# Three products of rounded and low parts in place of a plain fp32 product, in two recurrence steps of seven heads

## The reference

```python
S = exp(b_last)[..., None] * S + einsum('bhsk,bhsv->bhkv', kc * exp(b_last - bcum), vc)   # keys by values
o = einsum('bhts,bhsv->bhtv', A, vc) + einsum('bhtk,bhkv->bhtv', qc * exp(bcum), S)       # scores by values + queries by state
o = rms_norm(o, g_onorm);  y = (o * silu(z)) @ w_out
```

## Time and profile before

| | |
|---|---|
| median of 3 runs | 1036.03 us (1035.98 to 1036.13) |
| the profiled execution, its own time | 1035.79 us |
| its span in the trace | 1033.9 us |
| TensorE busy | 1025.0 us, 99% |
| VectorE busy | 705.3 us, 68% |
| ScalarE busy | 425.8 us, 41% |
| granted TensorE clock, mean | 0.999 |

### The profile page before, as it was taken

The page is one execution under the profiler, slowest core; times in us unless marked ns, Lnnn a source line. Parts: engine busy times, 40 slices in busy tenths (PEclk is TensorE's granted clock), DMA queues, the critical chain, the costliest instruction groups (busy, mean ns, idle before and its releaser), DMA issues.

```text
span 1033.9 us, 20543 instructions
## 1 busy us (share of the span) xinstructions
PE 1025.0 (99%) x7979; PEld 976.8 (94%) x7979; DVE 705.3 (68%) x1274; ACT 425.8 (41%) x860; POOL 18.3 (2%) x45
## 2 busy tenths in 40 slices
PE   8999999999999999999999999999999999999998
PEld 7999999999999978889999999999999999997886
DVE  6899777677776926762867768485776848586355
ACT  7444333332433614443345444434534344383222
POOL 1000000000000000000000000000000000000000
PEclk9999999999999999999999999999999999999999
DMA  8003121112111243321112211211221122143064
GB/s 253 22 22 82 42 77 46 41 43 79 41 41 61 102 164 119 123 82 42 49 55 64 62 28 56 63 54 48 62 61 41 42 63 61 57 152 111 23 241 171
DMA packets 95552, 78.75 MB, mean 76 GB/s; under 512 B 2965, under 2 KB 86886, under 8 KB 95510
## 3 DMA queue, kind: packets, MB, share of 16 engines
q1 hardware_dynamic: 77622, 69.19, 21.2%
q10 hardware_dynamic: 17888, 8.98, 3.0%
HBM read 64.72 MB, written 13.44 MB: 76 GB/s over the span
## 4 chain that ended last, share of the span: by engine, by line
PE 98%; DVE 1%; DMA 1%; ACT 0%; issue 0%; SPq 0%; DVEq 0%
PE bank L678 36%; PE bank L728 28%; PE bank L816 14%; PE bank L703 5%; PE bank L1066 4%; PE bank L910 2%; PE bank L1022 1%; PE bank L1015 1%; PE bank L1024 1%; PE bank L926 1%; PE bank L798 1%; PE bank L918 1%; PE bank L1010 1%; PE bank L833 1%; PE bank L974 1%; PE bank L905 1%
## 5 line engine op out<-in xcount | busy, mean ns | idle before, releaser
L678 PE MATMUL bank<-reg_a,wsplit 128*128 128x352 f32 x2304 | 381.5, 324 | 0.0
L678 PEld LDWEIGHTS bank<-reg_a,wsplit 128*128 128x128 f32 x2304 | 368.6, 188 | 1.1
L728 PE MATMUL bank<-reg_a,wsplit 128*128 128x264 f32 x1344 | 165.7, 284 | 0.0
L728 PEld LDWEIGHTS bank<-reg_a,wsplit 128*128 128x128 f32 x1344 | 164.1, 188 | 0.2 <-DVE arena L1901 0.2
L728 PE MATMUL bank<-reg_b,w_ring 128*128 128x264 f32 x1008 | 124.6, 284 | 0.0
L728 PEld LDWEIGHTS bank<-reg_b,w_ring 128*128 128x128 f32 x1008 | 123.3, 188 | 0.0
L816 PE MATMUL bank<-reg_b,reg_a 128*128 128x512 f32 x288 | 69.3, 396 | 0.0
L816 PEld LDWEIGHTS bank<-reg_b,reg_a 128*128 128x128 f32 x288 | 53.7, 188 | 12.6 <-issue 0.4
L1929 DVE TENSOR_TENSOR arena<-arena,bank 128x264 f32<-128x264 f32 x84 | 34.8, 427 | 34.2 <-PE bank L728 33.0
L1288 ACT ACTIVATE arena<-bank 128x264 f32<-128x264 f32 x84 | 32.2, 390 | 55.2 <-PE bank L728 50.5
L1266 ACT ACTIVATE w_ring<-wraw 128x512 fp32r<-128x512 f32 x42 | 26.1, 631 | 69.0 <-PE bank L728 69.0
(11 more groups left out here) (299 smaller groups left out, 1498.6 us busy)
## 6 DMA issues: line engine op xcount, KB each, us to landing
wraw<-in_w_in SPq DMA_DIRECT2D x64, 512.0 KB, 4.1
first_x<-in_x_prompt SPq DMA_DIRECT2D x8, 512.0 KB, 8.4
wraw<-in_w_out SPq DMA_DIRECT2D x8, 512.0 KB, 3.5
w_out_raw<-in_w_out SPq DMA_DIRECT2D x8, 512.0 KB, 5.2
arena<-in_w_out SPq DMA_DIRECT2D x8, 512.0 KB, 4.7
arena<-in_x_prompt SPq DMA_DIRECT2D x8, 512.0 KB, 3.4
x_scratch<-arena SPq DMA_DIRECT2D x8, 512.0 KB, 2.6
arena<-in_state_hgrn ACTq DMA_DIRECT2D x8, 512.0 KB, 3.9
```

Of the source, the lines that this page charges most:

```text
L678: mm = nc.tensor.matmul(bank[b][:, 0:CH], w[wi][:, k, :], rhs[hi], start=(k == 0 and i == 0), stop=(k == KT - 1 and i == 2))
L728: mm = nc.tensor.matmul(bank[banks[q]][:, 0:QT], w[wi][:, k, :], B_OP[name][hi][:, k, q * QT:(q + 1) * QT], start=(start and k == 0 and i ...
```

## The change

For the seven heads of the loop, the eight keys-by-values products of step 9 and the eight scores-by-values products of step 10 become three float32r matmuls each. The queries-by-state products (L1024) stay plain fp32, and so does the whole last head. The rounded parts are written by ScalarE, the low parts by VectorE, into columns of the arena that are done with at that point (an alias `rounded` of the arena as float32r, and three functions that give the place of a chunk's two parts). New events tell of them: `kta`, `kt`, `vha`, `vhb`, `aha`, `ahb` of ScalarE and `kla`, `klb`, `vla`, `vlb`, `ala`, `alb` of VectorE (k keys, v values, a scores). The scores are split in two pieces: chunks 0 and 1 (`EARLY`) in step 8, the other six in step 9, where their rounded parts take the place of the keys' rounded parts.

```diff
+        rounded = nc.alloc_sbuf_tensor_at("arena_rounded", [P, ARENA], F32R, offset=arena_at)
+        AT_KT, AT_K = CK * P, (2 * CK + 1) * P
...
+        EARLY = 2
...
+            def three_terms(dst, w, x, stop):
+                for i, (wi, xi) in enumerate(((0, 0), (1, 0), (0, 1))):
+                    mm = nc.tensor.matmul(dst, w[wi], x[xi], start=(i == 0), stop=(stop and i == 2))
+                return mm
...
+                elif s == 9 and not final:
+                    for c in range(CK):
+                        if c % 4 == 0:
+                            pe.wait_ge(VR.sem, VR.at(h, ("vla", "vlb")[c // 4]))
+                        mm = three_terms(bank[5 + c // 4][:, tokens(c % 4)], split_keys(c), split_values(c), True)
+                    mm.then_inc(PR.now("u"), 1)
...
-                        mm = nc.tensor.matmul(dst, r_am[:, tokens(c)], r_vt[:, tokens(c)], start=True, stop=(c == 0))
+                        if final:
+                            mm = nc.tensor.matmul(dst, r_am[:, tokens(c)], r_vt[:, tokens(c)], start=True, stop=(c == 0))
+                        else:
+                            if c == EARLY:
+                                pe.wait_ge(VR.sem, VR.at(h, "alb"))
+                            mm = three_terms(dst, split_scores(c), split_values(c), c == 0)
...
+                elif s == 8 and not final:
+                    act.wait_ge(PR.sem, PR.at(h, "kt"))
+                    for half in range(2):
+                        A(rounded[:, AT_KT + half * 512:AT_KT + (half + 1) * 512], bank[5 + half][:, :],
+                          ACT.Copy).then_inc(AR.now(("kta", "kt")[half]), 1)
+                    for half in range(2):
+                        A(rounded[:, AT_K + half * 512:AT_K + (half + 1) * 512], r_vt[:, half * 512:(half + 1) * 512],
+                          ACT.Copy).then_inc(AR.now(("vha", "vhb")[half]), 1)
+                    act.wait_ge(moved32, h + 1)
+                    A(rounded[:, AT_F + T - EARLY * P:AT_F + T], r_am[:, 0:EARLY * P], ACT.Copy).then_inc(AR.now("aha"), 1)
+                elif s == 9 and not final:
+                    act.wait_ge(PR.sem, PR.at(h, "u"))
+                    A(rounded[:, AT_KT:AT_KT + (CK - EARLY) * P], r_am[:, EARLY * P:], ACT.Copy).then_inc(AR.now("ahb"), 1)
...
+            def low_part(dst, src, hi):
+                return V.tensor_tensor(dst, src, hi.bitcast(F32), ALU.subtract)
```

More of the change, by code:

```diff
@@ L219, in build, with part_at, split_keys, split_values @@
         r_qb = sb("r_qb", [P, (2 * NB + 1) * NS])
+        rounded = nc.alloc_sbuf_tensor_at("arena_rounded", [P, ARENA], F32R, offset=arena_at)
+        AT_KT, AT_K = CK * P, (2 * CK + 1) * P
+        AT_Q = AT_K + T
+        AT_F, AT_KR = AT_Q + T, AT_Q + 3 * T
+        AT_VT = AT_Q + 6 * T
+        EARLY = 2
+        def part_at(at):
+            return rounded[:, at:at + P]
+        def split_keys(c):
+            return part_at(AT_KT + c * P), part_at(AT_F + CH + c * P if c < 3 else AT_KR + CH + (c - 3) * P)
+        def split_values(c):
+            return part_at(AT_K + c * P), part_at(AT_VT + c * P)
+        def split_scores(c):
+            return part_at(AT_F + T - (EARLY - c) * P if c < EARLY else AT_KT + (c - EARLY) * P), part_at(c * P)
         STK = 3 * NSAMP
@@ L328, in build @@
         GATED = ["lb", "v3", "qc", "k", "fa", "f", "tt", "g4", "g3", "ri", "i3", "i2", "i1", "kq", "vl", "vs"]
-        ENDED = [f"s{c}" for c in range(CK)] + ["r0", "r1", "rs", "on0", "on1", "ons"]
+        STATES = [f"s{c}" for c in range(CK)]
+        ENDED = ["r0", "r1", "rs", "on0", "on1", "ons"]
+        LOWS = ["kla", "klb", "vla", "vlb", "ala"]
         VR = Events(sem("rec_dve"), GATED + ["u2", "w4", "u4", "qb", "k3c", "kl", "as", "w8", "u8", "w16", "u16", "am", "w32", "c8",
-                                             "u32", "ss", "sn0", "snew", "w64", "c16", "u64"] + ENDED,
+                                             "u32", "ss", "sn0", "snew", "w64", "c16", "u64"]
+                    + LOWS + STATES + ["alb"] + ENDED,
                     GATED + ["u2", "am", "as", "w4", "u4", "qb", "k3c", "w8", "c8", "u8", "kl", "w16", "c16", "u16",
-                             "w32", "u32", "ss", "sn0", "snew", "w64", "u64"] + ENDED)
-        AR = Events(sem("rec_act"), ["gc", "vh", "vt", "sv", "kts", "qr", "kr", "os", "sqs", "q32", "k32", "kt", "sq0", "sq1", "sd"],
+                             "w32", "u32", "ss", "sn0", "snew", "w64", "u64"] + STATES + ENDED)
+        AR = Events(sem("rec_act"), ["gc", "vh", "vt", "sv", "kts", "qr", "kr", "os", "sqs", "q32", "k32", "kta", "kt",
+                                          "vha", "vhb", "aha", "ahb", "sq0", "sq1", "sd"],
                     ["gc", "vh", "vt", "sv", "kts", "os", "sqs", "q32", "k32", "kt", "sq0", "sq1", "sd"])
@@ L2403, in rec @@
                     join(h, 64, tl, tr)
+                elif s == 8 and not final:
+                    dve.wait_ge(AR.sem, AR.at(h, "kta"))
+                    low_part(rounded[:, AT_F + CH:AT_F + CH + 3 * P], bank[5][:, 0:3 * P], rounded[:, AT_KT:AT_KT + 3 * P])
+                    low_part(part_at(AT_KR + CH), bank[5][:, 3 * P:], part_at(AT_KT + 3 * P)).then_inc(VR.now("kla"), 1)
+                    dve.wait_ge(AR.sem, AR.at(h, "kt"))
+                    low_part(rounded[:, AT_KR + CH + P:AT_KR + CH + 5 * P], bank[6][:, :],
+                             rounded[:, AT_KT + 512:AT_KT + 1024]).then_inc(VR.now("klb"), 1)
+                    for half in range(2):
+                        dve.wait_ge(AR.sem, AR.at(h, ("vha", "vhb")[half]))
+                        cols = slice(half * 512, (half + 1) * 512)
+                        low_part(rounded[:, AT_VT:AT_VT + CK * P][:, cols], r_vt[:, cols],
+                                 rounded[:, AT_K:AT_K + CK * P][:, cols]).then_inc(VR.now(("vla", "vlb")[half]), 1)
+                    dve.wait_ge(AR.sem, AR.at(h, "aha"))
+                    low_part(rounded[:, 0:EARLY * P], r_am[:, 0:EARLY * P],
+                             rounded[:, AT_F + T - EARLY * P:AT_F + T]).then_inc(VR.now("ala"), 1)
                 elif s == 9:
@@ L2417, in rec @@
                         ins.then_inc(VR.now(f"s{c}"), 1)
+                    if not final:
+                        dve.wait_ge(AR.sem, AR.at(h, "ahb"))
+                        low_part(rounded[:, EARLY * P:CK * P], r_am[:, EARLY * P:],
+                                 rounded[:, AT_KT:AT_KT + (CK - EARLY) * P]).then_inc(VR.now("alb"), 1)
                 elif s == 10:
```

## The result

| | before | changed |
|---|---|---|
| median | 1036.01 us (4 runs) | 1048.2 us (4 runs, 1047.39 to 1048.54) |
| ratio to before | | 1.012, 95% interval 1.0108 to 1.0133 |
| the profiled execution, its own time | 1035.79 us | 1047.39 us |
| its span | 1033.9 us | 1045.5 us |

The change costs 12.2 us by the medians. The profiled execution is the shortest of the four, so its span grew by only 11.6.

The account below looks back on a forecast made before the run. TensorE's own work was taken as the bound almost everywhere. Steps 9 and 10 each add 0.86 us a head, +12.0 us over seven heads with the rest hidden, so 1036.03 becomes 1048.0 us; range 1046.0 to 1052.0, holding 0.84.

Parts of the forecast that it names:

- The price of a rounded matmul at 128 columns: TensorE, steps 9 and 10: 0.110 us each, set by the weight load; +0.86 us a step, +12.0 us in all.
- the line through the wide forms: Busy time over count at 264, 352 and 512 columns, carried down: streaming alone would take 0.060 us at 128 columns.
- The step before the change: Step 9's 16 plain records, taken off as 1.78 us, 0.111 us a record.
- The hidden work: Splitting by ScalarE and VectorE in steps 8 and 9: fits in their idle time and costs nothing.
- the late scores: Low part of the later scores in step 10: ready before TensorE asks, margin 0.4 to 0.5 us, the thinnest.
- The edges of the runs: TensorE's passages between plain and rounded runs: taken as nothing, at most 0.05 us a run, 0.7 us for 14 runs.
- A sign that I named wrongly: TensorE's matmul records: shorter than 275 ns at the same 0.11 us distance would be the mark of a load bound.
- Streaming as the bound: Rival in steps 9 and 10: loads run ahead freely, 0.060 us a matmul, -4.8 us, 1031.2 us; chance 0.05.
- Partly hidden loads: Rival in steps 9 and 10: load begins before its predecessor is through, pace say 0.084, +3.3, 1039.3 us; chance 0.05.
- The waits: Rival: late low or rounded parts stop TensorE some 0.5 us a head, +3.5 us, 1051.5 us; chance 0.08.
- The narrow form: Rival: a narrow rounded matmul works in two records like plain fp32, +50 us, 1086 us; chance 0.06.

Follow-up runs that it names:

- half a load: Changed kernel, but step 9's 24 rounded matmuls each load only 64 of 128 weight columns and stream all 128; 1040.1 us.
- half a stream: Changed kernel, but step 9's 24 rounded matmuls each stream only 64 of 128 columns, weights staying 128 x 128; 1048.28 us.
- the bf16 kernel: Changed kernel with rounded and low parts written as bf16 instead of float32r, same three terms with fewer digits; 1032.49 us, ratio 0.997 to the kernel before.
- splitting alone: Changed kernel with all parts and waits made, but each product one plain fp32 matmul of the rounded parts; 1036.01 us, ratio 1.0002 to the kernel before.

## Why the prediction was right

*The price of a rounded matmul at 128 columns* was the whole of it. It was taken from places in the trace where loads follow each other with little streamed between, and not from the length of a record, its busy time or the line through the wide forms. It was put at 0.110; the loads lie 0.112 apart, and the steps last 2.63 us (2.64 forecast) and 4.16 (4.2). 16 records of 0.111 in seven heads are 12.4 us; the medians differ by 12.2. The experiments with half a load and half a stream show the cause, and not just the size.

*The step before the change was read too long.* The 1.78 us that the prediction takes off run from the start of a matmul to the end of the next group's first load. From start to start, as the 2.63 are measured, step 9 took 1.70. By the starts of the loads, 1.83 us became 2.73: +0.90 a step where the forecast has +0.86, and 12.6 us in fourteen steps where it has 12.0. TensorE's busy time grew by just these 12.6. That 1048.0 met the median of 1048.2 so closely is in this part luck.

*Why a record costs what it did.* The prediction gives a rounded matmul and a plain record the same price, and the reason is not the same. The rounded one waits for its load. A plain one also streams for 0.11 us, twice as long as a rounded one over the same 128 columns. In the bf16 kernel a bf16 matmul behind a plain record starts 0.11 us after it, in all 42 places, although one bf16 matmul follows another after 0.056 and its own load had begun together with the plain record (load at 601.13, matmul at 601.24, above). In the kernel before, plain products with only eight weight columns, four side by side, take 0.11 us a round too (16 records in the 0.44 us from 576.33 to 576.77):

```profile
576.33 0.62 PE L947 MATMUL bank<-arena,r_qb 128*8 128x128 f32 x16
576.77 0.40 PE L950 MATMUL bank<-arena,r_as 128*8 128x128 f32 x8
```

So at 128 columns the stream of a plain record is as long as a load. That the two prices are equal is a coincidence of this size and does not carry over to wider products.

*The hidden work* stayed hidden, as splitting alone shows. ScalarE had 0.48 us to spare where I had 0.3, the late scores 0.55 where I had 0.4 to 0.5; one chunk less of lead used that up.

*The edges of the runs* cost nothing that the trace shows: the first load of the next group still follows the last one of step 9 by 0.11 us (599.39 to 599.50).

*A sign that I named wrongly:* I wrote that a load-bound matmul would show as a record shorter than 275 ns. It doesn't. Groups of the changed kernel:

```profile
L989 PE MATMUL bank<-arena_rounded 128*128 128x128 f32 x336 | 47.2, 276 | 0.0
L989 PEld LDWEIGHTS bank<-arena_rounded 128*128 128x128 f32 x336 | 42.7, 192 | 0.0
```

The matmul's record begins while its own load is still running and contains the rest of it. With half the load it is 222 ns, 54 less. With half the stream it stays at 273. A plain record is 275 ns long and has its long stream in it instead. So a length of 275 does not say by itself what bounds a matmul; a change of one of the two did.

*The rivals.* Streaming as the bound (1031.2) was refuted for four-byte weights, and came true for bf16. Partly hidden loads (1039.3) did not occur. The waits did not bite at `EARLY = 2`. The narrow form cost no second record.

The Trainium skill, "TensorE: Matmul & The Clock Gate", section LDWEIGHTS (loading the stationary operand), puts a load at its columns over 1.2 GHz, which makes 107 ns for 128 (an estimate), and names no type; the four-byte loads here agree with 112 and the bf16 loads, 0.02 apart, don't. The section Back-to-back issue gap of the same page gives 81 ns a matmul of 128 columns for sustained pairs; neither kind comes near it here (112 and 56 ns), and the measurement decides.

## What to carry to other kernels

Count the weight loads and not only the passes. A plain fp32 product is two loads and two streams, each stream twice as long as a rounded one; three rounded products are three loads and three short streams. They pay only where those streams hide the loads, and at 128 streamed columns they don't. By the rows here (two plain streams at some 1.7 ns a column in all, three loads at 0.336 us) the break would lie near 200 streamed columns; that is an estimate, and no run tried it. Read a load's price where nothing streams beside it. Where stationary tiles are used once and narrow, two-byte parts hide the loads behind even 128 columns, if their digits suffice; then keep them apart from four-byte products, since each change back exposes half a load.

## What the runs showed of the hardware that I had not expected

Halving the streamed columns of a load-bound rounded matmul left not only its time but also its record as it was (273 ns against 276). Two bf16 loads started 0.02 us apart against 0.11 for four-byte ones, a factor of five or more and not the two that the bytes suggest. A plain fp32 record streams 128 columns in 0.11 us, as long as its load, where a rounded one needs 0.060. A plain fp32 load behind a bf16 stream costs 0.055 us each time the type changes: 2.7 us in the bf16 version, which gained 3.2.
